# Moving the loads of each expert's second matrix from the sync engine's queue to GpSimd's own queue

## The chip, the cores and the metric

The kernel runs on one core of one Trainium2 chip. The metric is the device time of one execution in microseconds (us); lower is better. Times given as a median are over three executions of the same kernel.

## The reference

One decoder layer over 256 tokens of width 1024, all in float32. An attention block comes first (a projection of the normalised input, eight heads of forgetting attention, four heads of differential attention, an output projection, a residual). Then comes the part that matters here, a mixture of 32 experts of which each token uses 4, and last a gated embedding.

```python
def clamped_swiglu(h):
    x_glu = jnp.minimum(h[..., ::2], SWIGLU_LIMIT)
    x_lin = jnp.clip(h[..., 1::2], -SWIGLU_LIMIT, SWIGLU_LIMIT)
    return x_glu * jax.nn.sigmoid(SWIGLU_ALPHA * x_glu) * (x_lin + 1.0)
...
    def block_fn(args):
        tok, e = args
        xb = xs[tok]
        hb = clamped_swiglu(xb @ w1[e] + b1[e])
        return hb @ w2[e] + b2[e]
...
        h = h + mixed @ w_out[i]
        h = h + moe(rms_norm(h, g_mlp[i]), w_router[i], b_router[i], w1[i], b1[i], w2[i], b2[i])
        gate = jax.nn.sigmoid(rms_norm(h, g_ple[i]) @ w_ple_gate[i])
        h = h + gate * (p[i] @ w_ple_proj[i])
```

Each expert has a first matrix `w1[e]` (1024 x 2048, 8 MiB) and a second one `w2[e]` (1024 x 1024, 4 MiB), so the 32 experts are 384 MiB of weights that are read once from HBM.

## The kernel before

**Stages.** The attention block fills roughly the first 190 us. Then the router picks the experts and the kernel goes through 32 items, one per expert, two to a pass of the loop `pair`; an item gathers up to 64 tokens. (Further items would exist if an expert had more tokens than 64; with these inputs there are none.) After the ninth pair TensorE does a small piece of the last stage. After the last item come the norm and the gate product with `w_ple_gate`.

**An item on TensorE.** First the bias (L783), then the product with `w1` in eight pieces of 1 MiB, c = 0 to 7 (L792), each 128 rows of the matrix, one 8 KiB row to a partition. Then, while VectorE and ScalarE compute the SwiGLU, TensorE does other work: in the first item of a pair the combine of finished outputs (L730) and transposes, in the second the gathers for the next pair (L722). Then a transpose of the hidden values (L817), and the product with `w2` in four pieces of 1 MiB, c = 8 to 11 (L831), each two 4 KiB rows to a partition.

**The ring.** `ring` has twelve slots of 1 MiB, slot c for piece c of every item. TensorE raises `chunk_used` by one after each piece in the order 0 to 11; the load of piece c of item e waits until piece c of item e-1 was used, `chunk_used` >= (e-1)*12 + c+1. Each slot has its own semaphore `chunk_loaded[c]`, on which TensorE waits. Five pieces of item 1 go to other tiles (`wide` and `aT`) so that they can start earlier.

**Who issues.** The sync engine (SP, `@block.sync`) issues all of these loads in the order 0 to 11 of each item: L296 the pieces of `w1`, L299 those of `w2`. Behind the last item it issues the 4 MiB load of `w_ple_gate` into `wide` (L340), then the stores of the output. ScalarE issues small loads at the start. GpSimd (`@block.gpsimd`, named POOL in the profile) does the powers of the norms (`power`, L370), two transfers for a bias table (L377 and L384), index tables and memsets. From its power at about 192 us to its next one at 1163 us it does nothing.

Of the kernel before, what the change touches and what calls it, by code (L numbers as in the profile page):

```python
# [21 lines left out]
P = 128  # L22
# [3 lines left out]
KD = D // P  # L26
# [14 lines left out]
E = 32  # L41
# [3 lines left out]
EXTRA = T * TOPK // SLOTS  # L45
ITEMS = E + EXTRA
COLS = ITEMS + 2
RING = 12
# [47 lines left out]
def build(nc, a, out):  # L96
    with ExitStack() as ctx:
# [130 lines left out]
        def rows(ap):  # L228
            return ap.rearrange("(k p) n -> p k n", p=P)
# [45 lines left out]
        @block.sync  # L275
        def _(sp):
            x, pe_in = a["x"][0], a["p"][0, 0]
            for tt in range(TT):
                sp.dma_start(hres[:, tt, :], x[tt * P:(tt + 1) * P, :]).then_inc(x_loaded[tt], 16)

            for c in range(RING):
                g, half = c // 2, c % 2

                if c == 0:
                    sp.wait_ge(s["vec_loaded"], 16 * 5)
                if c == 2:
                    sp.wait_ge(s["wf_loaded"], 16 * 2)
                    sp.wait_ge(s["head_loaded"], 16 * 11)
                src = rows(w_in[half * 512:(half + 1) * 512, GROUP_COL[g]:GROUP_COL[g] + GROUP])
                sp.dma_start(ring[:, c, :].rearrange("p (k n) -> p k n", k=4), src).then_inc(win_loaded[c], 16)  # L290
            sp.dma_start(wide[:, :, :], rows(a["w_out"][0])).then_inc(s["wout_loaded"], 16)

            def load(e, c, dst):

                if c < KD:
                    sp.dma_start(dst, w1[e, c * P:(c + 1) * P, :]).then_inc(chunk_loaded[c], 16)  # L296
                else:
                    j = c - KD
                    sp.dma_start(dst.rearrange("p (k n) -> p k n", k=2),  # L299
                                 rows(w2[e, 2 * j * P:2 * (j + 1) * P, :])).then_inc(chunk_loaded[c], 16)  # L300

            def load_item(e, before, chunks=range(RING)):
                for c in chunks:
                    before(c)
                    load(e, c, ring[:, c, :])


            load_item(0, lambda c: sp.wait_ge(s["proj_done"], 2 * (c // 2) + 2))
            sp.wait_ge(s["pv_done"], 8)
            sp.wait_ge(s["sc_done"], 8)  # L310
            sp.wait_ge(s["b1_cleared"], 1)
            sp.dma_start(b1r[0:E, :], a["b1"][0]).then_inc(s["b_loaded"], 16)
            sp.dma_start(b2r[0:E, :], a["b2"][0]).then_inc(s["b_loaded"], 16)

            sp.wait_ge(s["out_done"], 4)
            for c in range(4):
                load(1, c, early[c])
            sp.wait_ge(s["logitsT_done"], TT)
            load(1, 4, early[4])
            sp.wait_ge(s["b_used"], 1)  # L320
            sp.dma_start(wp, rows(a["w_ple_proj"][0])).then_inc(s["tail_loaded"], 16)
            sp.dma_start(pin, pe_in.rearrange("(t p) n -> p t n", p=P)).then_inc(s["tail_loaded"], 16)

            for c in range(EARLY):
                sp.wait_ge(chunk_loaded[c], 32)
                sp.wait_ge(s["chunk_used"], c + 1)
                load(2, c, ring[:, c, :])
            load_item(1, lambda c: sp.wait_ge(s["chunk_used"], c + 1), range(EARLY, RING))
            load_item(2, lambda c: sp.wait_ge(s["chunk_used"], RING + c + 1), range(EARLY, RING))
            with sp.Fori(3, E) as e:  # L330
                load_item(e, lambda c: sp.wait_ge(s["chunk_used"], (e - 1) * RING + (c + 1)))
            sp.wait_ge(s["tables_ready"], 1)
            n = sp.value_load(ints[0:1, EXTRA:EXTRA + 1], min_val=0, max_val=EXTRA)
            with sp.If(n > 0):
                with sp.Fori(0, (n + 1) // 2 * 2) as i:
                    e = sp.value_load(ints[0:1, bass.ds(i, 1)], min_val=0, max_val=E - 1)
                    load_item(e, lambda c: sp.wait_ge(s["chunk_used"], (i + (E - 1)) * RING + (c + 1)))

            sp.wait_ge(s["chunk_used"], RING + EARLY)
            sp.dma_start(wide[:, :, :], rows(a["w_ple_gate"][0])).then_inc(s["gate_loaded"], 16)  # L340
            for q, (tt, c0, n) in enumerate(PARTS):
                sp.wait_ge(s["y_final"], q + 1)
                sp.dma_start(out[0, tt * P:(tt + 1) * P, c0:c0 + n], xn[:, tt, c0:c0 + n]).then_inc(s["stored"], 16)
            sp.wait_ge(s["stored"], 16 * len(PARTS))

        @block.gpsimd
        def _(pool):
            g = nc.gpsimd
            tn = Turns(pool, s["pool_turn"])
            g.memset(mhalf, -0.5).then_inc(s["mhalf_made"], 1)  # L350
            g.memset(ident[:, :], 0.0).then_inc(s["pool_turn"], 1)
            g.memset(ones[:, :], 1.0).then_inc(s["pool_turn"], 1)
            g.memset(fmask, 0.0).then_inc(s["pool_turn"], 1)
            tn.n = 3
            pool.wait_ge(s["pool_turn"], 3)
            g.affine_select(out=ident[:, :], in_=ident[:, :], compare_op=ALU.not_equal, fill=1.0, base=0,
                            pattern=[[-1, P]], channel_multiplier=1).then_inc(s["consts_made"], 1)
            g.affine_select(out=upper[:, :], in_=ones[:, :], compare_op=ALU.is_ge, fill=0.0, base=0,
                            pattern=[[1, P]], channel_multiplier=-1).then_inc(s["consts_made"], 1)
            g.affine_select(out=fmask[:, P:T], in_=fmask[:, P:T], compare_op=ALU.is_ge, fill=NEG, base=0,  # L360
                            pattern=[[-1, P]], channel_multiplier=1).then_inc(s["consts_made"], 1)
            pows = {"norm": [(ssq[:, tt:tt + 1], rstd[:, tt:tt + 1]) for tt in range(TT)],
                    "qk": [(ms, qr)], "sub": [(dms, dr)]}
            k = 0

            def power(src, dst):
                nonlocal k
                k += 1
                pool.wait_ge(s["mean_ready"], k)
                g.tensor_tensor(dst, src, mhalf[:, 0:src.shape[1]], ALU.pow).then_inc(s["pow_done"], 1)  # L370

            for pair in pows["norm"]:
                power(*pair)


            pool.wait_ge(s["vrow_ready"], 1)
            pool.dma_start(skew[:, :].rearrange("p (h n) -> h p n", h=DIFF_HEADS),  # L377
                           spread(vrow[0:DIFF_HEADS, :], 1, P)).then_inc(s["skew_stored"], 16)
            n = DIFF_HEADS * VROW
            back = bass.AP(skew.tensor, skew.offset + P - 1, [[n - 1, P], [VROW, DIFF_HEADS], [1, T]])  # L380
            for step, i in ORDER:
                if (step, i) == ("proj", 6):
                    pool.wait_ge(s["skew_stored"], 16)
                    pool.dma_start(t5, back).then_inc(s["t5_loaded"], 16)  # L384
                if step == "proj" and i in QK_UNITS:
                    power(*pows["qk"][0])
                if step == "pv" and i >= 8:
                    power(*pows["sub"][0])
            pool.wait_ge(s["pv_done"], 12)
            pool.wait_ge(s["sc_masked"], 16)  # L390

            g.iota(iota1, [[1, SLOTS]], base=1, channel_multiplier=0,
                   allow_small_or_imprecise_dtypes=True).then_inc(s["iotas_made"], 1)
            g.iota(iotae, [[1, E]], base=0, channel_multiplier=0,
                   allow_small_or_imprecise_dtypes=True).then_inc(s["iotas_made"], 1)
            g.iota(iota16, [[1, EXTRA]], base=0, channel_multiplier=0,
                   allow_small_or_imprecise_dtypes=True).then_inc(s["iotas_made"], 1)
            g.iota(iotap, [[0, 1]], base=0, channel_multiplier=1,
                   allow_small_or_imprecise_dtypes=True).then_inc(s["iotas_made"], 1)

            g.memset(arena[:, 1056:4128], 0.0).then_inc(s["b1_cleared"], 1)
            g.memset(GT, 0.0).then_inc(s["gt_cleared"], 1)

            g.memset(outs, 0.0).then_inc(s["out_taken"], 2)
            g.memset(SGT, 0.0).then_inc(s["sgt_taken"], 1)
            for pair in pows["norm"]:
                power(*pair)
            for pair in pows["norm"]:
                power(*pair)

# [858 lines left out]
```

## Time and profile before

| what | value |
|---|---|
| median of three executions | 1198.63 us (1197.98 to 1201.33) |
| span of the profiled execution, first to last instruction | 1199.4 us |
| TensorE matmul busy | 1097.4 us, 91% |
| VectorE, ScalarE, GpSimd busy | 17%, 13%, 2% |
| HBM read | 427.27 MB, 358 GB/s over the span |
| mean granted TensorE clock | 0.984 |
| loads of ring pieces | 379 of 1 MiB, 20.7 us from issue to landing |

For the profiled execution the profile gives the span alone; no device time of its own stands beside it. The span lies 0.8 us above the median and within the three times. A share of busy time is a mean over stages: what limits one stretch can stand idle in another.

### The profile page before, as it was taken

What the parts mean: (1) busy time and instruction counts of PE and PEld (TensorE: products, weight loads), DVE (VectorE), ACT (ScalarE), POOL (GpSimd) and SP (SyncE); (2) the same over time, 40 slices, a digit from 0 to 9 for tenths busy, and PEclk for the clock granted to TensorE, in tenths of its full rate; (3) what the DMA queues carried; (4) which work ended last, traced back from release to release, by engine and by line L of the source; (5) the groups of instructions that cost most, each with busy time, mean ns of one, the idle gap of its engine ahead of it and who ended that gap; (6) DMA issues with size and microseconds to landing.
All of it is one profiled execution on the core that took longest, in us unless ns stands there. A gap on an engine that the chain in (4) does not pass through costs nothing.

```text
span 1199.4 us, 13087 instructions
## 1 busy us (share of the span) xinstructions
PE 1097.4 (91%) x4957; PEld 456.2 (38%) x4957; DVE 209.0 (17%) x492; ACT 161.1 (13%) x316; POOL 27.6 (2%) x39
## 2 busy tenths in 40 slices
PE   7399978999999999999999998999999999999978
PEld 4156545443434343333333333343433333333334
DVE  2014335111111111111111112111111111111132
ACT  2033331001101010101010101010101010101010
POOL 1011020000000000000000000000000000000000
PEclk9699988999999999999999999999999999999999
DMA  7594304879999999999999999999999999999970
GB/s 207 155 402 168 141 13 175 331 278 414 417 418 418 418 418 418 418 418 417 418 418 418 417 418 418 416 417 418 418 418 418 418 417 418 417 418 417 418 305 35
DMA packets 86223, 429.38 MB, mean 358 GB/s; under 512 B 10648, under 2 KB 11217, under 8 KB 53405
## 3 DMA queue, kind: packets, MB, share of 16 engines
q1 hardware_dynamic: 81744, 427.45, 87.8%
q0 software_dynamic: 848, 1.32, 0.8%
q10 hardware_dynamic: 3612, 0.37, 0.2%
q8 instruction: 12, 0.20, 0.1%
q14 instruction: 7, 0.05, 0.0%
HBM read 427.27 MB, written 1.84 MB: 358 GB/s over the span
## 4 chain that ended last, share of the span: by engine, by line
PE 49%; DMA 26%; SPq 17%; issue 3%; DVE 3%; ACT 2%; ACTq 0%; POOL 0%; POOLq 0%; DVEq 0%
DMA ring<-in_w 23%; PE hidden L792 16%; PE outputs L831 10%; SPq L296 9%; SPq L299 7%; PE sum L600 6%; PE sum L730 4%; DMA ring<-in_w_in 3%; PE sum L585 2%; PE hidden L783 2%; PE tokens L722 2%; PE hidden L870 1%; ACT arena L530 1%; PE hidden L852 1%; PE tokens L870 1%
## 5 line engine op out<-in xcount | busy, mean ns | idle before, releaser
L792 PE MATMUL hidden<-ring,arena 128*64 128x512 f32 x2008 | 448.6, 595 | 26.1 <-DMA ring<-in_w 26.1
L792 PEld LDWEIGHTS hidden<-ring,arena 128*64 128x64 f32 x2008 | 138.9, 137 | 330.4 <-issue 249.5
L831 PE MATMUL outputs<-ring,arena 128*64 128x512 f32 x1024 | 226.8, 595 | 11.6 <-ACT arena L530 11.6
L1173 DVE TENSOR_SCALAR arena<-hidden 128x512 f32<-128x512 f32 x32 | 22.1, 691 | 741.2 <-PE hidden L792 741.2
L831 PEld LDWEIGHTS outputs<-ring,arena 128*64 128x64 f32 x1024 | 70.7, 137 | 145.3 <-issue 127.9
L600 PE MATMUL sum<-ring,aT 128*128 128x512 f32 x192 | 87.3, 609 | 18.9 <-DMA ring<-in_w_in 18.9
L525 ACT ACTIVATE arena<-arena 128x512 f32<-128x512 f32 x32 | 20.1, 629 | 509.7 <-DVE arena L1173 509.7
L722 PE MATMUL tokens<-arena,xn 128*128 128x128 f32 x544 | 71.0, 285 | 0.2
L722 PEld LDWEIGHTS tokens<-arena,xn 128*128 128x128 f32 x544 | 64.5, 195 | 17.1 <-issue 13.0
L730 PE MATMUL sum<-arena 128*128 128x512 f32 x136 | 62.9, 605 | 1.4 <-ACT arena L534 1.4
L783 PE MATMUL hidden<-arena 128*64 128x512 f32 x256 | 60.5, 593 | 1.6 <-DVE arena L1201 1.6
L600 PEld LDWEIGHTS sum<-ring,aT 128*128 128x128 f32 x192 | 36.8, 195 | 61.5 <-issue 61.3
L533 ACT COPY arena<-outputs 64x512 f32<-64x512 f32 x32 | 18.5, 578 | 251.1 <-PE outputs L831 251.1
L370 POOL TENSOR_TENSOR small<-small 128x8 f32<-128x8 f32 (+2 forms) x18 | 19.3, 1070 | 1131.3 <-DVE small L898 988.9
L730 PEld LDWEIGHTS sum<-arena 128*128 128x128 f32 x136 | 24.4, 189 | 39.6 <-issue 39.6
L817 PE MATMUL outputs<-ident,arena 128*128 128x128 f32 x128 | 20.0, 279 | 16.3 <-DVE arena L1178 16.3
L783 PEld LDWEIGHTS hidden<-arena 128*64 128x64 f32 x256 | 18.2, 137 | 37.9 <-issue 37.8
L585 PE MATMUL sum<-wide,aT 128*128 128x512 f32 x64 | 31.1, 637 | 0.9 <-ACT aT L452 0.9
L1118 DVE TENSOR_TENSOR arena<-tokens,gcols 128x512 f32<-128x512 f32 x34 | 23.4, 687 | 36.1 <-PE tokens L722 36.1
L530 ACT COPY arena<-outputs 128x512 f32<-128x512 f32 x32 | 18.8, 588 | 36.7 <-PE outputs L817 36.7
L1178 DVE TENSOR_TENSOR arena<-arena 128x512 f32<-128x512 f32 x32 | 22.1, 692 | 4.2
L1175 DVE SCALAR_TENSOR_TENSOR arena<-arena 128x512 f32<-128x512 f32 x32 | 22.1, 692 | 1.1
(238 smaller groups left out, 492.9 us busy)
## 6 DMA issues: line engine op xcount, KB each, us to landing
ring<-in_w SPq DMA_DIRECT2D x379, 1024.0 KB, 20.7
ring<-in_w_in SPq DMA_DIRECT2D x12, 1024.0 KB, 14.3
wide<-in_w_out SPq DMA_DIRECT2D x1, 4096.0 KB, 24.3
wide<-in_w SPq DMA_DIRECT2D x4, 1024.0 KB, 9.2
wide<-in_w_ple_gate SPq DMA_DIRECT2D x1, 4096.0 KB, 27.6
hres<-in_x SPq DMA_DIRECT2D x2, 512.0 KB, 4.7
aT<-in_w SPq DMA_DIRECT2D x1, 1024.0 KB, 7.3
arena<-in_w_ple_proj SPq DMA_DIRECT2D x1, 1024.0 KB, 5.0
```

The source lines that it names most:

```text
L296: sp.dma_start(dst, w1[e, c * P:(c + 1) * P, :]).then_inc(chunk_loaded[c], 16)
L299: sp.dma_start(dst.rearrange("p (k n) -> p k n", k=2), rows(w2[e, 2 * j * P:2 * (j + 1) * P, :])).then_inc(chunk_loaded[c], 16)
L530: c.copy(hT.rearrange("p k c -> p (k c)"), TB[:, :]).then_inc(s["hT_taken"], 1)
L585: ins = mm(B[q][:, :], aT[:, k, tt * P:(tt + 1) * P], wide[:, k, half * 512:(half + 1) * 512], start=(k == 0), stop=(k == KD - 1))
L600: ins = mm(B[i % 2][:, :], aT[:, k, tt * P:(tt + 1) * P], ring[:, 2 * g + k // 4, (k % 4) * GROUP:(k % 4 + 1) * GROUP], start=(k == 0), st ...
L722: ins = mm(GB[:, k * P:(k + 1) * P], xn[:, tt, (4 * b + k) * P:(4 * b + k + 1) * P], Sel[:, tt, :], start=(k == 0 and tt == 0), stop=(tt = ...
L730: ins = mm(Y[q][:, :], SGT[:, half, tt * P:(tt + 1) * P], outs[:, half, :], start=False, stop=False, skip_group_check=True)
L783: mm(H[u * SLOTS:(u + 1) * SLOTS, g * 512:(g + 1) * 512], expert1[:, i * SLOTS:(i + 1) * SLOTS], b1r[:, c0:c0 + 512], start=True, stop=False)
L792: ins = mm(H[u * SLOTS:(u + 1) * SLOTS, g * 512:(g + 1) * 512], xsel[:, k, i * SLOTS:(i + 1) * SLOTS], chunk(k, i)[:, c0:c0 + 512], start= ...
L831: ins = mm(TB[u * SLOTS:(u + 1) * SLOTS, :], hT[:, k % 4, (k // 4) * SLOTS:(k // 4 + 1) * SLOTS], chunk(c, i)[:, c0:c0 + 512], start=(k == ...
L870: ins = mm(gate_bank(tt, c0, n), aT[:, k, tt * P:(tt + 1) * P], wide[:, k, c0:c0 + n], start=(k == 0), stop=(k == KD - 1))
L1118: v.tensor_tensor(xsel[:, 4 * b:4 * b + 4, :], GB[:, :].rearrange("p (k c) -> p k c", k=4), spread(gcols[:, KD + 4 * b:KD + 4 * b + 4], 2, P),
```

## The change

The four pieces of `w2` of each item are issued by GpSimd on its own queue, each behind the same wait for its slot as before. The sync engine issues the eight pieces of `w1` alone, and behind those of the last item `w_ple_gate`. The tiles, the semaphores that the loads raise, and what TensorE waits for stay as they are. For item 0 GpSimd issues at the step `("out", 0)` of its walk through the attention order, for the others in a loop after its powers of the second norm and before those of the third.

```diff
@@ sync engine
             def load(e, c, dst):
-                if c < KD:
-                    sp.dma_start(dst, w1[e, c * P:(c + 1) * P, :]).then_inc(chunk_loaded[c], 16)
-                else:
-                    j = c - KD
-                    sp.dma_start(dst.rearrange("p (k n) -> p k n", k=2),
-                                 rows(w2[e, 2 * j * P:2 * (j + 1) * P, :])).then_inc(chunk_loaded[c], 16)
-
-            def load_item(e, before, chunks=range(RING)):
+                sp.dma_start(dst, w1[e, c * P:(c + 1) * P, :]).then_inc(chunk_loaded[c], 16)
+
+            def load_item(e, before, chunks=range(KD)):
...
-            load_item(1, lambda c: sp.wait_ge(s["chunk_used"], c + 1), range(EARLY, RING))
-            load_item(2, lambda c: sp.wait_ge(s["chunk_used"], RING + c + 1), range(EARLY, RING))
+            load_item(1, lambda c: sp.wait_ge(s["chunk_used"], c + 1), range(EARLY, KD))
+            load_item(2, lambda c: sp.wait_ge(s["chunk_used"], RING + c + 1), range(EARLY, KD))
@@ GpSimd
+            def load_down(e, c):
+                j = c - KD
+                pool.dma_start(ring[:, c, :].rearrange("p (k n) -> p k n", k=2),
+                               rows(w2[e, 2 * j * P:2 * (j + 1) * P, :])).then_inc(chunk_loaded[c], 16)
...
+                if (step, i) == ("out", 0):
+                    for c in range(KD, RING):
+                        pool.wait_ge(s["proj_done"], 2 * (c // 2) + 2)
+                        load_down(0, c)
...
+            with pool.Fori(1, E) as e:
+                for c in range(KD, RING):
+                    pool.wait_ge(s["chunk_used"], (e - 1) * RING + (c + 1))
+                    load_down(e, c)
+            pool.wait_ge(s["tables_ready"], 1)
+            n = pool.value_load(ints[0:1, EXTRA:EXTRA + 1], min_val=0, max_val=EXTRA)
+            with pool.If(n > 0):
+                with pool.Fori(0, (n + 1) // 2 * 2) as i:
+                    e = pool.value_load(ints[0:1, bass.ds(i, 1)], min_val=0, max_val=E - 1)
+                    for c in range(KD, RING):
+                        pool.wait_ge(s["chunk_used"], (i + (E - 1)) * RING + (c + 1))
+                        load_down(e, c)
```

## Rows read from the trace of the kernel before

**Rows 1.** The page: the span in 40 slices, about 30 us each.
```profile
PE   7399978999999999999999998999999999999978
...
PEclk9699988999999999999999999999999999999999
DMA  7594304879999999999999999999999999999970
GB/s 207 155 402 168 141 13 175 331 278 414 417 418 418 418 418 418 418 418 417 418 418 418 417 418 418 416 417 418 418 418 418 418 417 418 417 418 417 418 305 35
```

**Rows 2.** Windows: length, busy PE, PEld, DVE, ACT, POOL; clock, DMA share, GB/s.
```profile
250.00:260.00 10.00, 9.34 (x52) 4.06 (x48) 2.43 (x4) 0.63 (x1) 0.00 (x0) 1.00 0.50 176
300.00:600.00 300.00, 285.35 (x1356) 108.62 (x1350) 38.66 (x70) 32.59 (x50) 0.00 (x0) 1.00 1.02 418
...
1162.00:1164.00 2.00, 1.17 (x3) 0.19 (x1) 1.74 (x6) 1.59 (x6) 0.55 (x1) 1.00 0.12 47
```

**Rows 3.** The waits: engine, line waited for, us in total, times, longest.
```profile
PE hidden L792 <- DMA ring<-in_w: 26.1, 53, 0.6
```

**Rows 4.** The chain in order of time: start us, us, work; two pairs.
```profile
299.58 13.76 PE hidden L792 x64
...
355.54 13.76 PE hidden L792 x64
```

**Rows 5.** TensorE's timeline, items 30 and 31: start us, us, work, [idle before <- releaser].
```profile
1113.35 1.94 PE L792 MATMUL hidden<-ring,arena 128*64 128x512 f32 x8 [0.55 <-DMA ring<-in_w]
...
1120.52 7.09 PE L831 MATMUL outputs<-ring,arena 128*64 128x512 f32 x32 [0.73 <-ACT arena L530]
...
1143.44 1.94 PE L792 MATMUL hidden<-ring,arena 128*64 128x512 f32 x8 [0.55 <-DMA ring<-in_w]
...
1151.03 7.09 PE L831 MATMUL outputs<-ring,arena 128*64 128x512 f32 x32
...
1164.85 1.06 PE L556 MATMUL sum<-ident,xn 128*128 128x128 f32 x8 [1.69 <-DVE xn L907]
```

**Rows 6.** The sync engine's timeline from item 31's loads to the gate's load.
```profile
1106.46 13.38 SPq L296 DMA_DIRECT2D ring<-in_w  x8
1122.63 12.39 SPq L299 DMA_DIRECT2D ring<-in_w  x4
1136.23 3.15 SPq L340 DMA_DIRECT2D wide<-in_w_ple_gate  x1
```

**Rows 7.** Windows of 3 us inside the saturated stretch.
```profile
503.00:506.00 3.00, 2.81 (x14) 0.83 (x14) 0.00 (x0) 0.00 (x0) 0.00 (x0) 1.00 1.02 426
...
515.00:518.00 3.00, 2.27 (x15) 1.22 (x15) 1.09 (x4) 1.07 (x2) 0.00 (x0) 1.00 1.02 407
```

**Rows 8.** GpSimd's load of the bias table (L384): issue ns, and time to landing.
```profile
L384 POOL DMA_DIRECT2D arena<-skew x1: 813/813/813, 71.6 to 71.6; - x1
...
DMA to landing us min/median/max: 8.6/8.6/8.6
```

**Rows 9.** DMA queues from 71 to 81 us: packets, MB, share of 16 engines.
```profile
q1 hardware_dynamic: 923, 3.49, 88.5%
q0 software_dynamic: 144, 0.52, 14.8%
```

**Rows 10.** GpSimd's timeline: the powers that follow the places of the new loads.
```profile
157.58 0.70 POOL L370 TENSOR_TENSOR small<-small 128x2 f32<-128x2 f32 x1 [32.28 <-DVE small L888]
...
1163.37 0.55 POOL L370 TENSOR_TENSOR small<-small 128x1 f32<-128x1 f32 x1 [970.72 <-DVE small L898]
```

**Rows 11.** Windows of 2 us around a fall of TensorE's clock.
```profile
158.00:160.00 2.00, 0.00 (x0) 0.00 (x0) 1.55 (x6) 0.00 (x0) 0.28 (x1) 1.00 0.02 4
...
162.00:164.00 2.00, 2.00 (x12) 2.00 (x11) 0.00 (x0) 0.71 (x3) 0.00 (x0) 0.50 0.00 0
...
170.00:172.00 2.00, 2.00 (x3) 0.67 (x2) 0.46 (x2) 0.00 (x0) 2.00 (x4) 0.50 0.00 0
```

**Rows 12.** VectorE's timeline: the only copy from SBUF to SBUF in a pair.
```profile
1148.18 0.22 DVE L1114 COPY arena<-arena 128x128 f32 x1
```

## The prediction

> **What bounds the kernel now.** I read the 40 slices first. TensorE is at 9 or 8 tenths from slice 9 on and nearly all of its clock is full, so it looks like the limit; but the lines for DMA say otherwise. From slice 10 to slice 38 the DMA engines are at 9 tenths and move 414 to 418 GB/s without a break [rows 1]. Taken as one window, 300 to 600 us shows a DMA share of 1.02 and 418 GB/s, while TensorE has 285.35 of 300 us of work [rows 2]. So I went to the waits: TensorE's first-matrix product waits 53 times for a ring load, 26.1 us in all and never longer than 0.6 us [rows 3]. Small waits, but regular. The chain in order of time gives the other pace: early on, when the loads are ahead, a pair of items takes 355.54 - 299.58 = 55.96 us, 27.98 us an item [rows 4]. Near the end an item takes 1143.44 - 1113.35 = 30.09 us [rows 5], and 12 MiB at 418 GB/s are 12.58 / 0.418 = 30.1 us. The loads need 30.1 us an item, TensorE 28.0. In its first items the kernel lives on what was loaded ahead, then it goes at the pace of the DMA engines, and what it ends on is the volume of bytes, not any issue.
>
> What the reader is to keep: the DMA engines are work-conserving here. From about 270 to 1162 us something is always queued on them, and the last bytes (the gate matrix) come in shortly after 1162 us, where the share falls to 0.12 [rows 2]. Before 270 us there was a stretch in which all slots were full (176 GB/s from 250 to 260 us [rows 2]).
>
> **The change part by part.**
>
> *The issues.* The sync engine's four issues of an item's second matrix last 12.39 us, its eight of the first 13.38 us [rows 6]. They last so long because the queue they go into is full, not because an issue costs that; the engines are saturated meanwhile, so taking 12.39 us an item from the sync engine gives 0. On GpSimd an issue is seen once in this form: 813 ns for 512 rows of 1 KiB [rows 8]. A piece of the second matrix has 256 rows of 4 KiB. At 0.8 us each, four are 3.2 us in an item of 30, on an engine with nothing else to do from 192 to 1163 us [rows 10]. If the cover were gone it would delay each piece by 0.8 us; the cover is the ring itself, as the piece is wanted 28 us after its slot is free (1122.63 to 1151.03 us [rows 5, 6]). 0.
>
> *What stands behind the new waits on GpSimd.* For item 0: the power at 157.58 us, for which GpSimd waited 32.28 us [rows 10]; the slots of item 0 come free with the attention's projections, before that. For the rest: the third norm's powers at 1163.37 us [rows 10]. The last slot wait ends in item 30's second product, which ends at 1120.52 + 7.09 = 1127.6 us [rows 5], 36 us before. 0 for both. The memsets and tables are ahead of the loop. The waits themselves are the same, and the old order of issue was already the order in which slots come free, so the gap of 250 to 260 us stays too.
>
> *The bytes.* The same bytes, the same row sizes. A stretch in which mostly 8 KiB rows move shows 426 GB/s, one with mostly 4 KiB rows 407 [rows 7]. Does a row cost more from GpSimd's queue? Beside the sync queue, its one load took 14.8% of 16 engines for 10 us, 23.7 engine-us for 0.52 MB [rows 9], or 45.5 an MB. 4 KiB rows cost 16 / 0.407 = 39.3, 8 KiB rows 37.6: 1.7 for 122 rows more an MB. By the same slope 1 KiB rows (733 more an MB than 4 KiB ones) come to 39.3 + 10.2 = 49.5. The measured 45.5 for 1 KiB rows is below that, so I take no surcharge. The bounds are 0 and the whole difference, 45.5 - 39.3 = 6.2 engine-us an MB: x 4.19 MB / 16 = 1.6 us an item, x 29.6 items (892 us / 30.1) = 48 us. Below nothing: if mixing hid the cost of the 4 KiB rows, all bytes would move at 426, 0.57 us an item less, 17 us in all.
>
> VectorE is the neighbour that could disturb GpSimd. In a pair there is a single copy from SBUF to SBUF, 0.22 us [rows 12]; if each of 16 delayed a piece fully, that were 3.5 us, and the slack of the pieces takes it: 0. The Trainium skill (SBUF — State Buffer, the box on the "DVE blocks DMA" trap) says that a load issued from GpSimd starves while VectorE runs such a copy, since its descriptors can't be written. It speaks against the change; by it the sum would be at most those 3.5 us higher.
>
> *The order.* This is what moves. With one queue, all of item 31's first matrix came in before any of its second. When its last piece is in, at 1143.4 us [rows 5], four pieces of the second matrix are still to come. With two queues an engine serves both in turn, and the second matrix, whose slots come free early, takes its part ahead of the first. TensorE needs the first matrix first. How much gets ahead: the first issue of item 31's second matrix is at 1122.63 us [rows 6], 9.3 us after item 30's last first-matrix piece arrived at 1113.35 [rows 5]; in the steady state item 31's comes 30.1 us after item 30's, so 20.8 us after that issue. If the engines alternate row by row, 4 KiB against 8 KiB, the second matrix gets a third, 139 GB/s, one piece in 7.5 us, and 20.8 / 7.5 = 2.8 pieces are in. At 407 GB/s a piece is 2.58 us, so the last first-matrix piece comes 2.8 x 2.58 = 7.1 us later than now. From there to the item's end TensorE needs 1151.03 + 7.09 - 1143.44 = 14.7 us as before [rows 5].
>
> This is paid once, not per item: the period stays 30.1 us, since both streams together fill the engines, and every item runs the same 7 us behind. Behind the last item nothing gives it back. The gate matrix, now queued right behind the last first-matrix piece instead of at 1136.23 us [rows 6], is in by 1162 us as before, and its product, which follows the transposes of 1164.85 us [rows 5], then starts later anyhow.
>
> The bounds. If the whole second matrix gets ahead: 4 x 2.58 = 10.3 us. If r pieces of it are left when the first is complete, they share with the gate matrix, and the last of them lands 2.58 r after 1162.2 - 10.3 = 1151.9 us; with one piece's work of 1.8 us the item ends at 1153.7 + 2.58 r, against 1158.1 now. The delay is the larger of 2.58 (4 - r) and 2.58 r - 4.4, least at r = 2.85: 3.0 us; for r = 4 it is 5.9. So 3.0 to 10.3, and I take the row-by-row value of 7.
>
> Sum: 0 + 0 + 0 + 7 = 7 us. The span is 0.8 us above the median, so I add to the median: 1198.6 + 7 = 1205.6 us.
>
> **The rivals.**
>
> *The engines favour the sync queue.* GpSimd's one load brought 0.52 MB in 8.6 us [rows 8], 61 GB/s or 15% of the traffic, in smaller rows. If the second matrix gets that little beside the first, TensorE waits for the second matrix instead, and the first runs ahead until its eight slots are full and leaves the engines to the other. The period is again 30.1 us, and the end 3.0 to 5.9 us later: about 1203. The Trainium skill (DMA: Bandwidth & Descriptors, Queues, rings and completion order) says that an engine switches queues only after a packet, of some 9 to 17 descriptors; if GpSimd's packets hold one row each, this case follows. Against it: the trace counts 923 packets in 3.49 MB of the sync queue [rows 9], a row or less each. Chance 0.15, over half of it under 3.6 us.
>
> *Faster: two queues move more.* If mixed rows all moved at the 426 GB/s of the 8 KiB rows [rows 7], 17 us are gained against the 7 lost: 1189. It decides from 421.3 GB/s on, where the gain is 7 us. For it: the 418 is a mean of 407 and 426, and the ratio of the sizes is the only cause in sight. Against: share 1.02 has no room [rows 2]. Chance 0.12, a third of it within 0.3%.
>
> *Software rows cost more.* Up to the 48 us above, 1254; from 0.12 us an item on it outweighs what I round. Chance 0.10.
>
> *TensorE's clock.* The waits of an item, now in pieces of 0.55 us [rows 5], may join into one of about 2.1 us (30.1 - 28.0), as first-matrix pieces come 3.8 us apart and only the last is late. The clock was at the lower level, 1.2 GHz, from 162 us to 172 us after TensorE had stood still from 158 to 160 us and was half busy behind that [rows 11]; a gap of 1.69 us in dense work left it at 2.4 GHz [rows 5]. Ten us at half clock cost 5 us, 2.9 more than the slack, on some 18 items (53 waits, three an item) 52 us: 1258. Chance 0.05.
>
> **How the numbers follow.** Forecast 0.58, favoured sync queue 0.15, more GB/s 0.12, dearer rows 0.10, clock 0.05. Slower by over 0.3% (3.6 us, about what a measurement tells from no change): 0.57 of the forecast, 0.06 of the favoured sync queue, 0.15 of the dearer rows and the clock = 0.78. Faster: 0.08. Same: 0.01 + 0.09 + 0.04 = 0.14. The forecast's own range is 1201.6 to 1208.9. The range for 8 in 10 reaches into the first two rivals and a partial surcharge: 1198 to 1222.
>
> **What would show it.** In the profile after: the software queue with 128 loads and 134 MB; the DMA line still at 418 over slices 10 to 38 and over 300 to 600 us; the wait for the last first-matrix piece of item 31 ending near 1150 instead of 1143.4; first-matrix waits fewer and longer; no wait at L831; GpSimd issues near 0.8 us. The forecast is wrong if 300 to 600 us shows under 416 or over 421 GB/s, if the clock leaves 1.00 there, or if the last first-matrix piece comes less than 3 us later.

## The result, and the profile after

The changed kernel takes 1208.88 us (median of four executions, 1206.34 to 1213.97); the kernel before, run beside it, 1198.31 us (four, 1196.92 to 1201.33). The ratio is 1.0091, 95% interval 1.0064 to 1.0117: slower, by 10.6 us. The forecast was 1205.6 us in a range of 1198 to 1222, slower with a chance of 0.78. Direction and range held; the loss was forecast as 7 us, and TensorE waits in another place than forecast.

The page of the kernel after, first its slices (beside [rows 1]), then the queues (packets, MB, share of 16 engines) and the issues of ring pieces:

```profile
PEclk9699989999999999999999999999999999999999
DMA  7593304879999999999999999999999999999940
GB/s 206 163 401 155 140 13 200 339 293 417 419 419 416 418 418 418 417 418 417 417 418 417 418 417 417 401 420 418 416 418 418 417 418 417 418 418 417 417 184 35
...
q1 hardware_dynamic: 46928, 293.23, 59.2%
q0 software_dynamic: 35664, 135.54, 28.8%
...
ring<-in_w SPq DMA_DIRECT2D x251, 1024.0 KB, 16.4
ring<-in_w POOLq DMA_DIRECT2D x128, 1024.0 KB, 17.5
```

The engines are as full as before, at 416 to 420 GB/s nearly everywhere; one slice, around 770 us, stands out with 401. So neither the volume nor the rate of the stream explains 10.6 us. The last bytes of weights come in at about 1161 us here and at about 1161.5 us before (66 and 217 GB/s from 1161 to 1162 us); counted from the start of item 0's first product, given below, the stream ends 948 us after it instead of 946. The waits of the whole execution (beside [rows 3]), and then TensorE's timeline from item 30's second product to the end of item 31 (beside [rows 5]; L808, L847 and L799 are the old L792, L831 and L783):

```profile
PEld outputs L847 <- DMA ring<-in_w: 52.1, 21, 4.2
...
PE outputs L847 <- DMA ring<-in_w: 34.8, 19, 3.3
```

```profile
1125.84 5.37 PE L847 MATMUL outputs<-ring,arena 128*64 128x512 f32 x24 [0.73 <-ACT arena L546]
1134.50 2.64 PE L847 MATMUL outputs<-ring,arena 128*64 128x512 f32 x8 [3.29 <-DMA ring<-in_w]
1136.92 2.93 PE L799 MATMUL hidden<-arena 128*64 128x512 f32 x8
1139.68 13.90 PE L808 MATMUL hidden<-ring,arena 128*64 128x512 f32 x64
...
1159.23 7.09 PE L847 MATMUL outputs<-ring,arena 128*64 128x512 f32 x32
```

No product waits for the first matrix any more (two of its weight loads do, 0.6 us in all). All waits are at the second product, and there at the last of its four pieces: three pieces run through (x24), then TensorE stands for up to 3.3 us. The last such wait of the kernel is in item 30 and ends at 1134.50 us; item 31 runs without any.

The time from the start of item 0's first product to the end of item 31 is the part that the change touches; I call it the expert part. What lies ahead of it differs by up to 5 us between executions of all these kernels, so I compare that part. Before: from 215.69 us to 1151.03 + 7.09 = 1158.12 [rows 5], 942.4 us. After: from 213.07 us to 1166.32, 953.2 us. 10.8 us longer, which is the difference of the medians. The two starts are here, first of the kernel before, then of the one after:

```profile
215.69 13.90 PE L792 MATMUL hidden<-ring,arena 128*64 128x512 f32 x64
```

```profile
213.07 13.90 PE L808 MATMUL hidden<-ring,arena 128*64 128x512 f32 x64
```

Why the last piece is late is in the landings. The four second-matrix pieces of item 30, one window of the issues each (KB, us from issue to landing), issued at 1100.7, 1102.4, 1104.1 and 1105.8 us:

```profile
ring<-in_w POOLq DMA_DIRECT2D x1, 1024.0 KB, 11.9
...
ring<-in_w POOLq DMA_DIRECT2D x1, 1024.0 KB, 17.5
...
ring<-in_w POOLq DMA_DIRECT2D x1, 1024.0 KB, 23.1
...
ring<-in_w POOLq DMA_DIRECT2D x1, 1024.0 KB, 28.6
```

They land at 1112.6, 1119.9, 1127.2 and 1134.4 us, 7.3 us apart. That is 144 GB/s, 34% of 418. The packets of the two queues say how the engines divide (a packet in this trace is one row of these loads; packets, MB, share of 16 engines from 1110 to 1114 us):

```profile
q1 hardware_dynamic: 151, 1.09, 65.5%
q0 software_dynamic: 150, 0.55, 34.4%
```

Equal numbers of rows, 8 KiB from one queue and 4 KiB from the other, so a third of the bytes for the second matrix. The piece that is wanted first among all that are under way gets a third of the engines, while the rest carries first-matrix pieces of item 31. Of these, four had landed by 1131.2 us, and the fifth, issued at 1115.67 us, follows 0.5 us behind item 30's last piece, at 1134.9:

```profile
ring<-in_w SPq DMA_DIRECT2D x1, 1024.0 KB, 19.3
```

At 3.8 us a piece that makes 4.9 pieces ahead of the one that TensorE stood for.

### The profile page after: what moved, and what is told of

It is laid out like the page before. It is cut to its first block, busy times and chain, and to the rows that moved or that the text cites. A ratio compares the mean times of both kernels' runs of the same rounds, so it can differ in the third digit from the quotient of the medians.

```text
span 1207.6 us, 13181 instructions
## 1 busy us (share of the span) xinstructions
PE 1097.1 (91%) x4957; PEld 461.0 (38%) x4957; DVE 209.2 (17%) x492; ACT 161.5 (13%) x316; POOL 119.3 (10%) x168
## 4 chain that ended last, share of the span: by engine, by line
DMA 47%; PE 46%; DVE 3%; issue 3%; ACT 1%; ACTq 0%; POOL 0%; POOLq 0%; DVEq 0%; SPq 0%
DMA ring<-in_w 43%; PE hidden L808 15%; PE outputs L847 11%; PE sum L616 6%; DMA ring<-in_w_in 3%; PE hidden L799 2%; PE tokens L738 2%; PE sum L746 2%; PE sum L601 2%; PE hidden L886 1%; PE hidden L868 1%; PE tokens L886 1%; DVE arena L1191 0%; DVE arena L1190 0%; DVE arena L1194 0%
## 5 line engine op out<-in xcount | busy, mean ns | idle before, releaser
L808 PE MATMUL hidden<-ring,arena 128*64 128x512 f32 x2008 | 436.3, 592 | 0.0
L847 PE MATMUL outputs<-ring,arena 128*64 128x512 f32 x1024 | 236.4, 609 | 46.5 <-DMA ring<-in_w 34.8
L808 PEld LDWEIGHTS hidden<-ring,arena 128*64 128x64 f32 x2008 | 144.4, 137 | 286.8 <-issue 286.2
L373 POOL DMA_DIRECT2D ring<-in_w x128 | 91.7, 717 | 872.8 <-PE outputs L847 857.7
L847 PEld LDWEIGHTS outputs<-ring,arena 128*64 128x64 f32 x1024 | 69.4, 137 | 186.6 <-issue 117.1
L799 PE MATMUL hidden<-arena 128*64 128x512 f32 x256 | 65.5, 635 | 1.6 <-DVE arena L1217 1.6
L799 PEld LDWEIGHTS hidden<-arena 128*64 128x64 f32 x256 | 20.2, 152 | 44.8 <-issue 44.7
```

Of the source, the lines that this page charges most:

```text
L373: pool.dma_start(ring[:, c, :].rearrange("p (k n) -> p k n", k=2), rows(w2[e, 2 * j * P:2 * (j + 1) * P, :])).then_inc(chunk_loaded[c], 16)
L799: mm(H[u * SLOTS:(u + 1) * SLOTS, g * 512:(g + 1) * 512], expert1[:, i * SLOTS:(i + 1) * SLOTS], b1r[:, c0:c0 + 512], start=True, stop=False)
L808: ins = mm(H[u * SLOTS:(u + 1) * SLOTS, g * 512:(g + 1) * 512], xsel[:, k, i * SLOTS:(i + 1) * SLOTS], chunk(k, i)[:, c0:c0 + 512], start= ...
L847: ins = mm(TB[u * SLOTS:(u + 1) * SLOTS, :], hT[:, k % 4, (k // 4) * SLOTS:(k // 4 + 1) * SLOTS], chunk(c, i)[:, c0:c0 + 512], start=(k == ...
```

## The experiments

The theory, put before the runs: the cost is the order of arrival, and it is paid at the end (order theory). The rival: each piece issued by GpSimd costs something wherever it is (software queue theory). Two smaller suspects were the earlier gate matrix and the clock. Every kernel was run beside the kernel before.

**1. The last two items back on one queue.** The sync engine issues the second matrices of items 30 and 31 again, in the old order, with semaphores of their own.

```diff
-            with sp.Fori(3, E) as e:
+            with sp.Fori(3, E - 2) as e:
                 load_item(e, lambda c: sp.wait_ge(s["chunk_used"], (e - 1) * RING + (c + 1)))
+            for e in range(E - 2, E):
+                for c in range(RING):
+                    sp.wait_ge(s["chunk_used"], (e - 1) * RING + (c + 1))
+                    ...
-            with pool.Fori(1, E) as e:
+            with pool.Fori(1, E - 2) as e:
```

> The second matrices of items 30 and 31 go back to the sync engine's queue, in the old order; items 0 to 29 stay on GpSimd's. Order theory (a second-matrix piece is served behind first-matrix pieces that are not yet wanted; paid once, at the end, where the last wait is that for item 30's last piece): the bytes of the last two items come in the old order, so the time is back within 2 us of the kernel before (ratio 0.998 to 1.002), though 30 of 32 items still use two queues. Software queue theory (each piece issued by GpSimd costs something): 30/32 of the loss stays, 9 to 10 us. As the prediction had it (first matrix of item 31 late): back to the time before too.

Measured: 1204.39 us, ratio 1.0047 (1.0030 to 1.0064), about half of the loss (6.0 us; 7.5 us on the expert part of the one profile, see the table). Both theories missed. TensorE's timeline in this kernel, items 29 to 31 (L859 is the second product):

```profile
1102.71 1.94 PE L859 MATMUL outputs<-ring,arena 128*64 128x512 f32 x8 [0.68 <-DMA ring<-in_w]
...
1125.33 7.09 PE L859 MATMUL outputs<-ring,arena 128*64 128x512 f32 x32 [0.73 <-ACT arena L556]
...
1153.52 7.09 PE L859 MATMUL outputs<-ring,arena 128*64 128x512 f32 x32
```

The waits for ring loads end in item 29, the last one on two queues, and items 30 and 31 go at TensorE's own pace: 1160.61 - 1102.71 = 57.9 us for one piece and two items, 28.0 us an item. In items 30 and 31, that is, it waits for no load: TensorE is *behind*, and with the old order it catches up no more than 30.1 - 28.0 = 2.1 us an item. That is a third form of the theory, a debt, and runs 9 and 10 test it.

**2. Only item 31 back on one queue.** As above with 1 for 2.

> Only item 31's second matrix goes back to the sync engine. Order theory with the last wait at item 30's last second-matrix piece: that wait stays as it is, since item 30 is still on two queues, so 7 to 10 us slower than before. The prediction's step (what costs is item 31's second matrix getting ahead of its first): nothing gets ahead in item 31 any more, so back within 2 us. Software queue theory: 8 to 10 us slower.

Measured: 1210.8 us, ratio 1.0101 (1.0061 to 1.0141). Nothing is cured, and the wait of item 30 is still there:

```profile
1135.08 3.33 PE L859 MATMUL outputs<-ring,arena 128*64 128x512 f32 x8 [3.46 <-DMA ring<-in_w]
```

The step of the prediction that puts the cost into item 31, whose second matrix gets ahead of its first, is refuted for this kernel.

**3. Everything through GpSimd's queue, in the old order.**

```diff
-            with sp.Fori(3, E) as e:
-                load_item(e, lambda c: sp.wait_ge(s["chunk_used"], (e - 1) * RING + (c + 1)))
...
+            load_item(3, lambda c: sp.wait_ge(s["chunk_used"], 2 * RING + (c + 1)))
...
+            with pool.Fori(4, E) as e:
+                pool_item(e, lambda c: pool.wait_ge(s["chunk_used"], (e - 1) * RING + (c + 1)))
...
+            pool.dma_start(wide[:, :, :], rows(a["w_ple_gate"][0])).then_inc(s["gate_loaded"], 16)
```

`pool_item` issues all twelve pieces of an item.

> One queue again, but GpSimd's: from item 4 on GpSimd issues all twelve pieces of an item in the old order, and the gate matrix behind them; the sync engine issues items 0 to 3. 336 pieces come through the software queue instead of 128. Order theory: within 3 us of the kernel before, 418 GB/s in the saturated stretch. Software queue theory: 336/128 of the loss, 25 us slower or more, and a lower GB/s.

Measured: 1197.86 us, ratio 0.9999 (0.9983 to 1.0014). Its window of 300 to 600 us (TensorE busy, weight loads, VectorE, ScalarE, GpSimd, clock, DMA share, GB/s) and its waits:

```profile
300.00:600.00 300.00, 284.55 (x1351) 108.61 (x1348) 39.18 (x71) 32.59 (x50) 73.97 (x126) 1.00 1.02 418
```

```profile
PE hidden L805 <- DMA ring<-in_w: 25.9, 53, 0.6
```

336 pieces from GpSimd, and still 418 GB/s, and the same 53 short waits as in [rows 3]. A cost of the software queue itself doesn't show; only the use of two queues costs.

**4. ScalarE's hardware queue in GpSimd's place.** ScalarE issues the next item's four pieces together, behind its copies of an item's outputs.

```diff
                     c.copy(outs[SLOTS:P, 1 - i, :], TB[SLOTS:P, :]).then_inc(s["out_taken"], 1)
+                    if down(i):
+                        for q in range(KD, RING):
+                            j = q - KD
+                            act.dma_start(ring[:, q, :].rearrange("p (k n) -> p k n", k=2),
+                                          rows(w2[2 * p + (i + 1), 2 * j * P:2 * (j + 1) * P, :])
+                                          ).then_inc(down_chunk[q], 16)
```

> The split stays, but ScalarE's hardware queue takes GpSimd's place from item 1 on: ScalarE issues the four pieces of the next item behind its copies of an item's outputs, when all four slots are free (up to 5 us later than GpSimd does). Order theory: slower than before by 8 to 15 us, with waits for the last second-matrix piece of up to 8 us. Software queue theory: no loss but what ScalarE's four issues cost it (2 us an item that nothing waits for): within 3 us of before.

Measured: 1235.02 us, ratio 1.029 (1.0254 to 1.0326), 37 us. The sign is that of the order theory, so it is not GpSimd; the size is over twice the 8 to 15 us expected. The page's GB/s line shows why:

```profile
GB/s 203 184 406 114 136 13 242 356 264 419 353 418 418 417 418 417 400 418 418 390 418 419 390 419 407 358 419 356 419 420 382 419 419 398 419 418 385 418 193 35
```

Now the engines themselves pause, in ten of the slices. The second matrix is asked for up to 5 us later, lands later, TensorE stands longer (up to 5.3 us), and meanwhile the sync engine's queue has filled all eight slots of the first matrix and has nothing left to do. One such place:

```profile
602.00:604.00 2.00, 2.00 (x6) 0.47 (x4) 0.00 (x0) 0.00 (x0) 0.00 (x0) 0.50 1.00 418
604.00:606.00 2.00, 2.00 (x8) 0.57 (x6) 0.00 (x0) 0.69 (x2) 0.00 (x0) 0.50 0.52 213
606.00:608.00 2.00, 2.00 (x10) 0.64 (x8) 0.00 (x0) 0.47 (x1) 0.00 (x0) 0.72 0.73 154
```

Nothing is asked for on the sync engine's queue between about 586 and 610 us, and its last piece lands at 606 us; ScalarE issues its first piece at 605.4 us. Over ten-us windows from 290 us on, what is missing to 418 GB/s adds up to 26 us. The other 13 of the 38.8 us that the expert part loses here were not taken apart. In the kernels with one queue, where the piece that TensorE waits for is the next to come, no slice from the 11th to the 38th is under 416 GB/s.

**5. 8 KiB rows for the second matrix, on two queues.** Partition p takes two neighbouring rows of `w2`, and the transposes take every second column of the hidden values to match.

```diff
-                pool.dma_start(ring[:, c, :].rearrange("p (k n) -> p k n", k=2),
-                               rows(w2[e, 2 * j * P:2 * (j + 1) * P, :])).then_inc(chunk_loaded[c], 16)
+                pool.dma_start(ring[:, c, :], w2[e, 2 * j * P:2 * (j + 1) * P, :].rearrange("(p k) n -> p (k n)", k=2)
+                               ).then_inc(chunk_loaded[c], 16)
...
-                        ins = tr(TB[:, k * P:(k + 1) * P], prod[:, k * P:(k + 1) * P], ident[:, :])
+                        ins = tr(TB[:, k * P:(k + 1) * P], prod[:, 256 * (k // 2) + k % 2:256 * (k // 2) + 256:2],
+                                 ident[:, :])
```

> The changed kernel with one more edit: a piece of the second matrix is read as 8 KiB rows (partition p takes two neighbouring rows of the matrix, and the transposes of the hidden values take every second column to match). If the engines alternate row by row, the second matrix now gets a half instead of a third beside the first: its pieces take 5 us instead of 7.5, the waits move from its last piece to the first matrix's last pieces. All bytes in 8 KiB rows: 423 GB/s or more in the saturated stretch, where a row size that costs nothing would leave 418. Time: 12 to 17 us from the rate against 7 to 10 for the order, 2 to 10 us faster than the kernel before.

Measured: 1201.63 us, ratio 1.0040 (1.0015 to 1.0065). The waits moved as expected. The waits of this kernel, and TensorE at the first product of item 31:

```profile
PE hidden L808 <- DMA ring<-in_w: 30.8, 18, 3.0
```

```profile
1141.33 1.94 PE L808 MATMUL hidden<-ring,arena 128*64 128x512 f32 x8 [3.02 <-DMA ring<-in_w]
```

With equal rows each queue gets half: the second-matrix pieces of item 30 land 5.0 us apart (at 1101.4, 1106.4, 1111.4 and 1116.4 us), 210 GB/s of 422. The second matrix comes early and the first late, at its last piece, and in item 31 as well. This is the place that the prediction had named for the changed kernel. So the share of each queue, which follows its row size, decides who waits. The time missed: it is slower than before, not faster, and the rate is 422 GB/s, not 423 or more.

**6 and 11. The same rows in the kernel before, one queue.** Run twice.

> The same 8 KiB rows in the kernel before, one queue, old order. Rate theory: 423 to 426 GB/s, an item in 29.5 us instead of 30.1, 10 to 17 us faster than the kernel before. If the 407 GB/s seen beside the second matrix were not due to its rows: no change. The difference between this run and the one with 8 KiB rows on two queues is the price of the order without the difference of row sizes: 5 to 10 us.

> The kernel before with 8 KiB rows of the second matrix once more, with more rounds: 7 to 9 us faster than before, from 422 instead of 418 GB/s: 372 MB x (1/418 - 1/422) = 8.4 us.

Measured: 1190.8 us, ratio 0.9939 (0.9917 to 0.9962), then 1188.98 us, 0.9919 (0.9902 to 0.9937). Faster than both kernels, by 7.3 and 10.0 us against the kernel before, where 10 to 17 and then 7 to 9 were expected. The window of 300 to 600 us of the second run:

```profile
300.00:600.00 300.00, 286.43 (x1368) 111.88 (x1364) 40.98 (x74) 33.22 (x51) 0.00 (x0) 1.00 1.01 422
```

422 GB/s, not the 426 that a stretch of first-matrix rows had shown in [rows 7]: the first expectation took a 3 us window for the rate of a row size. From 418 to 422 GB/s come the 8.4 us of the second one, which lie between the two measured gains. On the expert part, 932.7 and 933.5 us here against 945.4 in run 5: two queues cost 12 us with equal rows too, above the 5 to 10 expected. Run 5's slice around 770 us is at 377 GB/s, (1 - 377/422) x 30 = 3.2 us of it.

**7. The gate matrix later.**

```diff
-            sp.wait_ge(s["chunk_used"], RING + EARLY)
+            sp.wait_ge(s["chunk_used"], (E - 1) * RING + 1)
```

> The changed kernel, but the sync engine issues the gate matrix only once TensorE has used the first piece of item 31 (about 20 us later). If the gate matrix's bytes compete with the second matrices of items 30 and 31 for what TensorE waits on, this gains some of the 8 us; if, as the order theory has it, its bytes come behind the last wait anyway, within 2 us of the changed kernel, 7 to 10 us slower than before.

Measured: 1208.56 us, ratio 1.0091 (1.0070 to 1.0112), as the changed kernel. The gate matrix's time of issue is out of it.

**8. The changed kernel again.**

> The changed kernel as it is, beside the others on the same chip: 8 to 11 us slower than before, with the last wait at item 30's last second-matrix piece. If the fall of the clock behind such a wait is by chance, its place and length differ from the first profile while the waits are the same.

Measured: 1209.41 us, ratio 1.0096 (1.0073 to 1.0119), 11.3 us and so just above the 8 to 11 expected. The expert part is 953.2 us again, with 19 waits of 34.8 us in all, and the last in item 30:

```profile
1135.69 2.64 PE L847 MATMUL outputs<-ring,arena 128*64 128x512 f32 x8 [3.12 <-DMA ring<-in_w]
1138.11 2.93 PE L799 MATMUL hidden<-arena 128*64 128x512 f32 x8
```

The clock falls behind this wait in the same place as in the first profile and about as long. But the wait alone doesn't decide it: in the first profile the clock fell behind six of the 19 waits (2.1 to 3.3 us), and after three others of such length (2.15, 2.52 and 3.03 us) the products took their usual time. The longest of the three:

```profile
710.62 1.94 PE L847 MATMUL outputs<-ring,arena 128*64 128x512 f32 x8 [3.03 <-DMA ring<-in_w]
```

What decides between them was not found.

**9 and 10. The last four and the last six items back on one queue.** As run 1 with 4 and with 6.

> The second matrices of items 28 to 31 go back to the sync engine's queue. Debt theory (TensorE is some 11 us behind when the last item on two queues is done; with the old order behind it, it goes at its own 28.0 us an item against the engines' 30.1 and catches up 2.1 us an item, until it is back at the engines' pace): 11.5 - 4 x 2.1 = 3 us slower than before. If the old order at the end had been enough by itself, two items would have cured it; they did not.

> The second matrices of items 26 to 31 go back to the sync engine's queue; items 0 to 25 stay on two. Debt theory: 11.5 - 6 x 2.1 < 0, so TensorE is back at the engines' pace before the end, and what is left is only what the DMA engines themselves stood idle while slots of the first matrix were full (slice 26 of the changed kernel, 1 to 3 us): 0 to 3 us slower than before. If something is lost at every item on two queues: 26/32 of the loss, 8 us or more.

Measured: 1202.42 us, ratio 1.0029 (1.0012 to 1.0047), and 1202.45 us, 1.0032 (1.0017 to 1.0047). The timeline with six items, from item 25 on:

```profile
982.91 1.94 PE L859 MATMUL outputs<-ring,arena 128*64 128x512 f32 x8 [0.96 <-DMA ring<-in_w]
1005.61 7.09 PE L859 MATMUL outputs<-ring,arena 128*64 128x512 f32 x32 [0.80 <-ACT arena L556]
...
1033.79 7.09 PE L859 MATMUL outputs<-ring,arena 128*64 128x512 f32 x32
...
1107.67 1.94 PE L820 MATMUL hidden<-ring,arena 128*64 128x512 f32 x8 [0.18 <-DMA ring<-in_w]
```

The last wait of the two-queue kind is in item 25; then TensorE runs free for four items, and from 1107.67 us it is back at the short waits for the first matrix, as before. The debt is paid. With four items the first such wait comes in item 31, at 1144.58 us: the debt is just paid there too. An estimate from four items of 2.1 us is that it was some 8 us of the 11, not all of them. What remains, 3.5 us (2.7 to 3.3 on the expert part), doesn't fall from four items to six, so it is not debt. It is just above the 0 to 3 expected. Part of it is the dip of slice 26, here 389 GB/s where 418 would be full, (1 - 389/418) x 30 = 2.1 us of idle engines.

The expert part in all profiles:

| kernel | expert part, us | against 942.4 |
|---|---|---|
| before | 942.4 | |
| all through GpSimd, one queue | 942.3 | -0.1 |
| last six items on one queue | 945.1 | +2.7 |
| last four | 945.7 | +3.3 |
| last two | 949.9 | +7.5 |
| last one | 953.6 | +11.2 |
| changed (two profiles) | 953.2, 953.2 | +10.8 |
| gate matrix later | 952.0 | +9.6 |
| ScalarE's queue | 981.2 | +38.8 |
| 8 KiB rows, two queues | 945.4 | +3.0 |
| 8 KiB rows, one queue (two profiles) | 932.7, 933.5 | -9.7, -8.9 |

## Why the prediction was right in direction and short in size

**What bounds the kernel** held: 418 GB/s from 300 to 600 us after as before, and the end follows the transfers.

**The issues** held. GpSimd's issues took 0.72 us each where 0.8 was taken from [rows 8], and no wait of TensorE comes from them. **GpSimd's later work** held, 0. **The bytes** held, and run 3 shows it for 336 pieces instead of 128: no surcharge, no gain. The slope that explained the 45.5 engine-us was drawn from two 3 us windows and was too steep, since 8 KiB rows alone give 422 GB/s; the value taken, 0, was right all the same. **VectorE's copies**: 0, nothing seen.

**The order** was the right mechanism, its share was right (a third; 34% measured), and the place was wrong.

The step that failed: "20.8 / 7.5 = 2.8 pieces are in", and the conclusion that TensorE waits for item 31's first matrix and not at the second product. Item 31's last first-matrix piece did come later, at 1120.79 + 25.8 = 1146.6 us, which is 5.8 us later than before when both are counted from the start of item 0; but TensorE reaches it only at about 1151.8 us and doesn't wait, while at the second product it waits 19 times, 34.8 us in all. The conclusion rests on the second matrix being complete in time. At a third of the rate four pieces take 30.1 us, and I had 0.8 us for the issue; measured is 11.9 us to the first landing instead of 8.3, so item 30's last piece is in 33.7 us after the first issue (1134.4 - 1100.7). TensorE on its own pace would want it at 1131.2 us. So the second matrix is the late one.

Then the sum is another: 4.9 pieces of 2.51 us ahead of the one waited for, 12.3 us, less the 2.3 us of slack that it had in one queue, is 10.0 (that slack is from run 3: item 30's last piece is issued at 1094.86 us, lands 25.0 us later at 1119.9, and is used at 1122.2). With the 1.2 us for which the engines stood idle around 770 us (401 instead of 418 GB/s) it is 11.2. Measured, from the start of item 0 on: TensorE begins that piece after 1134.50 - 213.07 = 921.4 us, in run 3 after 1122.2 - 212.2 = 910.0, so 11.4 us later.

From that wait on, two small terms: TensorE catches up 2.1 us in item 31; the clock takes 1.7 (below); together -0.4. 11.4 - 0.4 = 11.0, against 10.8 on the expert part. In it are some 3 us that don't come back even with the old order behind (runs 9 and 10), of which the idle engines are 1.2 in the changed kernel and 2.1 in run 10; where the rest comes from stays open.

"Paid once, at the end" held in substance: 26 of 32 items on two queues cost 3.5 us, and the last six 7 more. But most of it is a debt of TensorE that is worked off at 2.1 us an item, not a shift that the old order in the last item undoes (runs 1 and 2). The claim that the engines always have work was nearly right: with two queues and eight slots ahead they can run dry, by 1 to 3 us around 770 us, and by 26 us when the second queue is asked late (run 4).

**The rivals.** "The engines favour the sync queue" had the right symptom, TensorE waiting for the second matrix, but not by that cause: the share was a third, not 15%, and the end came 10.8 us later, beyond its 3.0 to 5.9. "Two queues move more" is refuted by the 418 GB/s of the changed kernel, and "software rows cost more" by run 3. "The clock" was right in that waits join into longer ones and the clock falls behind some of them; its price was wrong, 1.7 us behind the last wait instead of 52 in all. That the five falls before it cost nothing, because TensorE would have waited again anyway, is argued and not shown.

**The gate matrix**: the bound for r pieces left treated item 31 alone; the last wait was an item earlier, where the gate matrix isn't yet under way, and run 7 shows that its time of issue doesn't matter.

## What to carry to other kernels

When a stream of loads is limited by bytes, one queue in the order of use is a schedule, and a second queue gives that up: here the engines took as many rows from one queue as from the other, and the piece that was wanted next got only its share, 34%. Check for each queue how long its burst takes at its share of the rate and when its last piece is wanted; and ask whether the other queue can fill its slots and leave the engines idle. What the change leaves on the table is in the rows: longer rows in the one queue gained 7 to 10 us where a second queue lost 11.

## What the runs showed of the hardware

- Two queues that are both full share the 16 engines by the number of rows: 4 KiB rows beside 8 KiB rows get 34% (a piece of 1 MiB every 7.3 us; 150 packets beside 151), and 8 KiB rows beside 8 KiB rows get half (a piece every 5.0 us, run 5), so that the waits change sides. The Trainium skill (DMA: Bandwidth & Descriptors, Queues, rings and completion order) says that an engine changes queues only behind a packet of some 9 to 17 descriptors; landings and counts would be the same for any equal number of rows a turn, so nothing here shows how many an engine takes.
- A stream that GpSimd issues moves as fast as one of the sync engine's: 418 GB/s with 336 pieces of 1 MiB, while VectorE and ScalarE work as always. The Trainium skill's warning that such loads starve beside VectorE's copies (SBUF — State Buffer, the "DVE blocks DMA" trap) doesn't show in these traces; with one copy of 0.22 us in a pair [rows 12] this kernel hardly tries it.
- 8 KiB instead of 4 KiB rows for a third of the bytes: 422 instead of 418 GB/s.
- The first piece of a burst on the second queue landed 11.9 us after its issue, though the next ones follow every 7.3 us; in run 5 it is 9.3 and 5.0. Where the 4.6 and 4.3 us go was not found.
- After the 3.3 us wait that ended at 1134.50 us, TensorE's clock went from 2.4 to 1.2 GHz in mid-work. The windows, before and behind:

```profile
1132.00:1134.00 2.00, 0.00 (x0) 0.00 (x0) 0.00 (x0) 0.00 (x0) 0.59 (x1) 1.00 1.02 418
...
1136.00:1138.00 2.00, 2.00 (x8) 0.72 (x6) 0.00 (x0) 0.81 (x2) 0.21 (x1) 0.50 1.01 414
```

Eight products took 2.64 us instead of 1.94 and the next eight 2.93 instead of 1.89, 1.7 us in all. A wait of 1.34 us in the same place (run 7) left both at 1.94 and 1.89; one of 3.03 us that ended at 710.62 us did so too (under run 8).
